# Hybrid block and two attention layers on one core: maxima spread by transfers, triangle products as first term, weights' splits moved or given to GpSimd

## The reference

```python
h = rms_norm(x, g); u, z_a, q, k, v, o, z_b, gates, g_a, g_b = split(h @ w_in)
y_a = (mix(window_means(u) - u) * pool_scale) * silu(z_a)
q, k = silu(conv5(q, k))
hb = mlstm(q, k, v, i, f) + flip(mlstm(flip(...)))        # 4 heads of 256
y_b = rms(hb) * g * sigmoid(o) * silu(z_b)
x = x + rms_norm((sigmoid(g_a) * (y_a @ Wa) + sigmoid(g_b) * (y_b @ Wb)) @ w_out)
# layer e: 6 heads with a window of 128, 6 heads with distance bias, 4 heads on the memory
# layer o: 12 heads with a forget bias (running sum of log sigmoid), 4 heads on the memory
x = x + (attention * silu(z)) @ w_out_layer
```

## Time and profile before

| | |
|---|---|
| median of 3 runs | 1219.95 us |
| lowest and highest run | 1217.41, 1223.23 us |
| the profiled execution's own time | 1218.77 us |
| its span, first to last instruction | 1216.9 us |
| TensorE busy | 1175.4 us, 97% |
| VectorE, ScalarE, GpSimd busy | 633.7, 568.6, 132.3 us |
| HBM read and written | 102.55 and 2.12 MB |

### The profile page before, as it was taken

How to read it: one execution, slowest core, us unless ns; L and a number is a source line. 1 busy time by engine, 2 the same in 40 slices (tenths; PEclk the granted TensorE clock), 3 DMA queues, 4 the chain that set the end, 5 groups by cost and what they waited for, 6 DMA issues and landing times.

```text
span 1216.9 us, 15215 instructions
## 1 busy us (share of the span) xinstructions
PE 1175.4 (97%) x5970; PEld 952.1 (78%) x5970; DVE 633.7 (52%) x1174; ACT 568.6 (47%) x1013; POOL 132.3 (11%) x146
## 2 busy tenths in 40 slices
PE   5999999999999999999999999899999999999998
PEld 4887888888876777788788888677788788877777
DVE  5485423588533454434547663787445565256631
ACT  4433431243335444544335565677434576366630
POOL 1000000000000000000000004334220000522522
PEclk9999999999999999999999999999999999999999
DMA  5233223332221221143335233212223233122221
GB/s 182 94 99 103 73 101 104 104 98 79 101 70 36 69 69 35 49 140 104 119 144 127 78 104 69 62 45 70 68 72 106 70 104 102 64 70 70 79 70 69
DMA packets 106703, 105.65 MB, mean 87 GB/s; under 512 B 17788, under 2 KB 92924, under 8 KB 106632
## 3 DMA queue, kind: packets, MB, share of 16 engines
q1 hardware_dynamic: 104984, 98.46, 25.8%
q10 hardware_dynamic: 1648, 6.23, 1.4%
HBM read 102.55 MB, written 2.12 MB: 86 GB/s over the span
## 4 chain that ended last, share of the span: by engine, by line
PE 90%; DVE 5%; ACT 3%; issue 1%; DMA 0%; DVEq 0%; ACTq 0%
PE acc L1522 23%; PE acc L1524 23%; PE acc L1523 23%; PE acc L1858 3%; PE aux L1884 3%; PE aux L1872 2%; PE aux L1696 2%; PE aux L1522 2%; PE aux L1524 2%; PE aux L1523 2%; PE aux L1710 2%; DVE wlo L995 2%; ACT whi L633 1%; PE acc L1863 1%; PE aux L1612 1%
## 5 line engine op out<-in xcount | busy, mean ns | idle before, releaser
L1522 PE MATMUL acc<-ht_hi,whi 128*128 128x512 f32 x736 | 293.4, 399 | 8.9 <-DVE wlo L995 7.9
L1523 PE MATMUL acc<-ht_lo,whi 128*128 128x512 f32 x736 | 287.8, 391 | 0.0
L1524 PE MATMUL acc<-ht_hi,wlo 128*128 128x512 f32 x736 | 287.7, 391 | 0.0
L995 DVE TENSOR_TENSOR wlo<-raw,whi 128x2048 fp32r<-128x2048 f32 x71 | 162.3, 2288 | 156.2 <-ACT whi L633 150.4
L1522 PEld LDWEIGHTS acc<-ht_hi,whi 128*128 128x128 f32 x736 | 139.0, 189 | 40.4 <-DVE wlo L995 9.3
L1523 PEld LDWEIGHTS acc<-ht_lo,whi 128*128 128x128 f32 x736 | 139.0, 189 | 30.0 <-issue 1.9
L1524 PEld LDWEIGHTS acc<-ht_hi,wlo 128*128 128x128 f32 x736 | 139.0, 189 | 29.3
L633 ACT ACTIVATE whi<-raw 128x2048 fp32r<-128x2048 f32 x71 | 135.3, 1910 | 50.8 <-DMA raw<-w_in_dram 22.9
L579 POOL TENSOR_SCALAR whi<-raw 128x512 fp32r<-128x512 f32 x64 | 43.4, 679 | 1029.0 <-DMA raw<-e_w_in_dram 758.7
L1522 PE MATMUL acc<-whi,ht_hi 128*128 128x512 f32 (+1 forms) x224 | 84.1, 375 | 0.8 <-DVE gbT L1246 0.8
L580 POOL TENSOR_TENSOR wlo<-raw,whi 128x512 fp32r<-128x512 f32 x64 | 83.4, 1303 | 5.3
(11 more groups left out here) (226 smaller groups left out, 1852.0 us busy)
## 6 DMA issues: line engine op xcount, KB each, us to landing
raw<-w_in_dram SPq DMA_DIRECT2D x72, 512.0 KB, 4.4
raw<-o_w_in_dram SPq DMA_DIRECT2D x28, 512.0 KB, 4.5
raw<-e_w_in_dram SPq DMA_DIRECT2D x14, 512.0 KB, 5.0
raw<-w_proj_pool_dram SPq DMA_DIRECT2D x8, 512.0 KB, 4.0
raw<-w_proj_mlstm_dram SPq DMA_DIRECT2D x8, 512.0 KB, 4.4
raw<-w_out_dram SPq DMA_DIRECT2D x8, 512.0 KB, 4.4
raw<-o_w_out_dram SPq DMA_DIRECT2D x8, 512.0 KB, 4.7
raw<-e_w_in_dram SPq DMA_DIRECT2D x14, 256.0 KB, 3.8
```

The lines of the kernel that those rows point to most:

```text
L995: v.tensor_tensor(wlo[:, slot, :], raw[:, slot, :], whi[:, slot, :].bitcast(F32), ALU.subtract).then_inc(w_split, 1)
L1522: mm(out_, w_hi_, x_hi, start=first, stop=False)
L1523: mm(out_, w_hi_, x_lo, start=False, stop=False)
L1524: return mm(out_, w_lo_, x_hi, start=False, stop=last)
```

## The change

- The maxima: after the scans VectorE signals `rowmax_ready`; SP stores the 64 x 512 rows to DRAM after the loads of w_proj_pool. After the loads of v it spreads head 0's two rows to 128 partitions into `rowmax_all`, and for each later head it does the same between the loads of O(h) and ZB(h), after waiting until all decay arguments of the head before are made. `rowmax_hi`, `rowmax_lo`, their split and the spreading products are gone, with two waits of TensorE. VectorE reads the maxima from `rowmax_all`.
- The triangles: `causal(p)` waits for the pair two before and, in layer o, writes the triangle products as the first term of the diagonal block. A step issues `causal` of both pairs, then the scores of both. Scores in layer o are cut at the diagonal block and are added.
- The rest of unit 1 is made ahead of the gate rows.
- The mix is evicted into eight tiles `mixT` of their own, without waiting for heads; the rest of g_a's second unit comes before the eight rests.
- In stage ozb the head and the rest of O(h+1) stand behind the head's normalisation, on both engines.
- The memory values' unit is split in iteration t = 1, and all first transposes stand after the first half of the values.
- GpSimd splits the first q/k unit of layer o.

```diff
@@ -148,12 +148,12 @@
         xnrow = at("xnrow", [P, TT, D], R0)
-        rowmax_hi = at("rowmax_hi", [64, S], CST + 7 * K, F32R)
-        rowmax_lo = at("rowmax_lo", [64, S], CST + 9 * K, F32R)
+        rowmax_all = at("rowmax_all", [P, 2, S], CST + 7 * K)
         zaT = at("zaT", [P, KT, S], R0)
...
         win_t = at("win_t", [P, 4, S], R3 + 5 * K)
+        mixT = at("mixT", [P, KT, S], R1)
         grow = at("grow", [P, 7, S], R2 + 2 * K)
@@ -190,6 +190,7 @@
 
+        rowmax_dram = nc.dram_tensor("rowmax_rows", (64, S), F32, kind="Internal").ap()
         csum_dram = nc.dram_tensor("csum_rows", (C_HEADS, S), F32, kind="Internal").ap()
@@ -228,12 +229,13 @@
         gm_ready = sem("gm_ready")
-        rowmax_split = sem("rowmax_split")
+        rowmax_ready = sem("rowmax_ready")
+        rowmax_out = sem("rowmax_out")
+        rowmax_in = sem("rowmax_in")
         last_rows = sem("last_rows")
...
         floor_ready = sem("floor_ready")
-        mbc_ready = sem("mbc_ready")
         s_ready = sem("s_ready")
@@ -324,7 +326,7 @@
 
-        BY_POOL = {plan["gates"][0], plan["o_f"][0]}
+        BY_POOL = {plan["gates"][0], plan["o_f"][0], plan["o_qk"][0]}
         for name in ("e_z", "e_out", "o_z", "o_out"):
@@ -478,11 +480,24 @@
             stage("pa", wview(A["w_proj_pool"][0]), 0)
+            sp.wait_ge(rowmax_ready, 1)
+            sp.dma_start(rowmax_dram, rowmax[:]).then_inc(rowmax_out, 16)
+
+            def spread_rowmax(h):
+                if h:
+                    sp.wait_ge(arg_ready, 2 * TT * h)
+                for d in range(2):
+                    r = 32 * d + h
+                    sp.dma_start(rowmax_all[:, d, :], rowmax_dram[r:r + 1, :].to_broadcast([P, S])).then_inc(rowmax_in, 16)
             stage("qk", W1, COL_QK)
             stage_wide("v", W1, COL_V, 4)
+            sp.wait_ge(rowmax_out, 16)
+            spread_rowmax(0)
             n = plan["ozb"][0]
...
                 load(W1, h * UC + COL_O, 2 * h + n)
+                if h:
+                    spread_rowmax(h)
                 load(W1, h * UC + COL_ZB, 2 * h + n + 1)
@@ -607,6 +622,7 @@
             split_narrow(plan["o_f"][0], C_HEADS, [(0, 0, C_HEADS)])
+            split(plan["o_qk"][0])
             for name in ("o_z", "o_out"):
@@ -707,7 +723,7 @@
             for j in range(KT):
-                head(win_t[:, j % 4, :], op_hi[:, j, :])
+                head(mixT[:, j, :], op_hi[:, j, :])
             weight_heads(n0 + 2)
@@ -780,7 +796,6 @@
                     evac(a, a % 2, half, ogT[:, 2 * h + half:2 * h + half + 1, :], ACT.Sigmoid)
-                weight_heads(n0 + 2 * h + 2)
                 for t in range(TT):
@@ -796,6 +811,7 @@
                 nc.scalar.activation(small[:, 8:12], small[:, 4:8], ACT.Exp, scale=-0.5).then_inc(hrs_ready, 1)
+                weight_heads(n0 + 2 * h + 2)
                 if h + 1 < HEADS:
@@ -848,7 +864,7 @@
                     root(t - 1)
-                if t == 2:
+                if t == 1:
                     weight_heads(n0 + 5)
@@ -1041,6 +1057,7 @@
             G = lambda i, lo=0, hi=64: grow[lo:hi, i, :]
+            weight_rests(1)
             dve.wait_ge(acc_ready, 2)
@@ -1089,10 +1106,9 @@
             step(v.tensor_tensor_scan(rowmax[32:64, ::-1], back, back, FLOOR, ALU.max, ALU.bypass))
+            dve.sem_inc(rowmax_ready, 1)
             v.tensor_tensor(G(5, 64, 128), G(4), rowmax[:], ALU.add).then_inc(gm_ready, 1)
             v.tensor_copy(ident_r[:], ident[:])
-            step(v.tensor_copy(rowmax_hi[:], rowmax[:]))
-            v.tensor_tensor(rowmax_lo[:], rowmax[:], rowmax_hi[:].bitcast(F32), ALU.subtract).then_inc(rowmax_split, 1)
             weight_rests(n0 + 5)
@@ -1108,15 +1124,14 @@
                     j = 2 * g + half
-                    dve.wait_ge(hi_ready, 8 + j - 3)
-                    tile_written(v.scalar_tensor_tensor(win_t[:, j % 4, :], acc[:, 2 * s + half, :], V("pool_scale", j),
+                    tile_written(v.scalar_tensor_tensor(mixT[:, j, :], acc[:, 2 * s + half, :], V("pool_scale", j),
                                                         zaT[:, j, :], ALU.mult, ALU.mult))
...
                 dve.sem_inc(acc_free, 1)
-                for j in (2 * g, 2 * g + 1):
-                    rest(win_t[:, j % 4, :], op_hi[:, j, :], op_lo[:, j, :])
-
             n0, _, _ = plan["ga"]
+            weight_rests(n0 + 1)
+            for j in range(KT):
+                rest(mixT[:, j, :], op_hi[:, j, :], op_lo[:, j, :])
             weight_rests(n0 + 3)
@@ -1170,9 +1185,9 @@
                     w = hi - lo
-                    dve.wait_ge(mbc_ready, h + 1)
+                    dve.wait_ge(rowmax_in, 32 * (h + 1))
                     mask = masks1[:, 0, 0:w] if d == 0 else masks1[:, 1, S - w:S]
-                    v.scalar_tensor_tensor(decay[:, seen["arg"] % 4, 0:w], aux[:, d, lo:hi], gcol[:, j, d, h:h + 1],
+                    v.scalar_tensor_tensor(decay[:, seen["arg"] % 4, 0:w], rowmax_all[:, d, lo:hi], gcol[:, j, d, h:h + 1],
                                            mask, ALU.subtract, ALU.max).then_inc(arg_ready, 1)
@@ -1197,7 +1212,6 @@
             for h in range(HEADS):
-                weight_rests(n0 + 2 * h + 2)
                 for t in range(TT):
@@ -1215,6 +1229,7 @@
                 ins.then_inc(hbn_ready, 1)
+                weight_rests(n0 + 2 * h + 2)
                 if h + 1 < HEADS:
@@ -1675,17 +1690,9 @@
                     pe.wait_ge(hb_ready, TT * h)
-                    if h > 1:
-                        pe.wait_ge(t_ready, 16 + 2 * (h - 1))
                 else:
...
                     pe.wait_ge(floor_ready, 2)
-                for d in range(2):
-                    r = 32 * d + h
-                    one_row = ident_r[0:64, r:r + 1].to_broadcast([64, P])
-                    mm(aux[:, d, :], one_row, rowmax_hi[0:64, :], start=True, stop=False)
-                    ins = mm(aux[:, d, :], one_row, rowmax_lo[0:64, :], start=False, stop=True)
-                ins.then_inc(mbc_ready, 1)
                 score_tiles(h, (0, 1))
@@ -1723,7 +1730,6 @@
             pe.wait_ge(consts_in, 32)
-            pe.wait_ge(rowmax_split, 1)
             scores(0)
@@ -1778,12 +1784,11 @@
                                 ins.then_inc(tr_ready, 1)
-                first_transposes(range(3))
                 n, a = n0 + 1, a0 + 1
...
                     if t:
-                        first_transposes((3,))
+                        first_transposes(range(TT))
                     for k in range(KT):
@@ -1846,22 +1851,29 @@
                 def logits(p):
+                    first = pairs[p][0]
+                    forget = first.bias is not None and first.bias[0] == "forget"
+                    ends = [c for c in range(2 * P, first.keys, 2 * P)] + [first.keys]
+                    if forget and first.keys - P not in [0] + ends:
+                        ends.insert(-1, first.keys - P)
+                    c = 0
+                    for end in ends:
+                        for e, job in enumerate(pairs[p]):
+                            (qt, qp), (kt_, kp) = job.q, job.k
+                            k0 = P * job.k0
+                            ins = mm(logit_bank(p, e)[:, c:end], qk[qp:qp + HD2, qt, P * job.t:P * job.t + P],
+                                     (mkT if job.bias is None else qk)[kp:kp + HD2, kt_, k0 + c:k0 + end],
+                                     start=not forget, stop=not forget or end == first.keys)
+                        c = end
+                    ins.then_inc(logit_ready, 1)
+
+                def causal(p):
+
                     if p >= 2:
                         pe.wait_ge(nm_ready if pairs[p - 2][0].bias is not None else pr_ready, 2 * (done + p - 1))
-                    first = pairs[p][0]
-                    forget = first.bias is not None and first.bias[0] == "forget"
-                    for c in range(0, first.keys, 2 * P):
-                        w = min(2 * P, first.keys - c)
-                        for e, job in enumerate(pairs[p]):
-                            (qt, qp), (kt_, kp) = job.q, job.k
-                            k0 = P * job.k0 + c
-                            ins = mm(logit_bank(p, e)[:, c:c + w], qk[qp:qp + HD2, qt, P * job.t:P * job.t + P],
-                                     (mkT if job.bias is None else qk)[kp:kp + HD2, kt_, k0:k0 + w],
-                                     start=True, stop=not (forget and c + w == job.keys))
-                    if forget:
-                        for e, job in enumerate(pairs[p]):
-                            ins = mm(logit_bank(p, e)[:, job.keys - P:job.keys], ident_r[:], causal_r[:], start=False, stop=True)
-                    ins.then_inc(logit_ready, 1)
+                    for e, job in enumerate(pairs[p]):
+                        if job.bias is not None and job.bias[0] == "forget":
+                            mm(logit_bank(p, e)[:, job.keys - P:job.keys], ident_r[:], causal_r[:], start=True, stop=False)
 
```

(2 more changed lines are left out.)

## The result

The changed kernel takes 1186.47 us, the median of four runs (1186.28 to 1189.16), against 1218.68 us of the kernel before beside it (1215.85 to 1223.23). The ratio is 0.9731 with an interval of 0.9706 to 0.9757. The forecast was 1191.5.

What follows compares the result with a forecast made beforehand. TensorE, busy 1175.4 of 1216.9 us, was taken as the bound. Terms 2.9 + 1.7 + 7.4 + 1.7 + 4.8 + 6.0 + 0.9 + 2.1 = 27.5 us off 1218.8 gave 1191.3, stated as 1191.5; range 1186 to 1201.

Steps and rivals of the forecast that it cites:

- split behind normalisation: Output gate's weight split after the head's normalisation: all four waits for `hrow` go, 7.4 us, at worst two thirds.
- maxima: Maxima spread by transfers: 1.22 us for each of three heads and 1.1 for the first, 4.8 together.
- triangles: Triangles as first term in layer o: 0.5 us in each of 12 steps, 6.0 us, at worst 4.0.
- first rest: First weight's rest ahead of the gate rows: u starts 2.9 us earlier; the clock's first fall, 1.7, counted separately.
- clock: Two of five half-clock stretches go, ahead of u and at the `hrow` wait: 1.7 us each, bounds 0 and 1.7.
- Rival B: Fewer clock falls than forecast: the three kept ones vanish too, 1186 us; chance 0.08.
- D: Values still wait, GpSimd is late, or late decay factors stop the scores: about 5 us less, 1196.5; chance 0.11.
- F: The maxima's broadcasts compete with weight loads, 512 KB more per head: 1193 us at most; chance 0.04.
- C: Triangles give little since VectorE's chain, not TensorE, sets the step: 6 us less, 1197.5; chance 0.1.
- E: Waiting for both pairs ahead of the scores closes a ring of late scores and VectorE minima: 1225 us; chance 0.01.
- Transposes and the GpSimd weight: Later transposes at layer e's memory values: 0.9 us, bounds 0 and 1.9; o_qk weight by GpSimd: 2.1, bounds 0 and 2.2.
- Rival A: The clock falls again in other places, behind remaining or new waits, two more falls: 1195 us; chance 0.2.

Runs made afterwards that it cites:

- four parts undone: Changed kernel with the first weight's rest, o_qk by GpSimd, later transposes and eight mixed tiles undone at once: 1198.3 us, ratio to before 0.9823.

## Why the prediction was right or wrong

Each row: what the prediction gave, what the traces' product starts gave, what undoing the part gave at full clock. The changed kernel stands at 1184.4 (eight runs).

| part | forecast | by starts | undone, full clock |
|---|---|---|---|
| split behind normalisation | 7.4 | 8.5 | 9.3 |
| maxima | 4.8 | 5.1 | 6.2 |
| triangles | 6.0 | 5.9 | 5.9 |
| first rest, GpSimd weight, transposes, tiles | 5.9 | 6.0 | 5.3 |
| sum without the clock | 24.1 | 25.5 | 26.7 |
| clock | 3.4 | 7.2 by the runs' mean clocks | |

At full clock the change is worth 1209.6 - 1184.4 = 25.2 us. The mean clock is known to 0.0005, 0.6 us in one run, and the start of the kernel varies by as much, so I take the last column as good to some 0.5 us a row; its sum is 1.5 above the 25.2, which four such errors can make. Within that the parts add up and none covers for another.

- **The falls of the clock: the step that failed.** Keeping three falls ("at most three stretches at 1.2 GHz") and 1.7 us each for two that go took the falls of one profiled execution as a property of the kernel. The runs of before lost 10.5 us to the clock on average (time multiplied by one minus the clock), those of the changed kernel 3.3: 7.2 us, not 3.4. By the medians it is 7.0: before lies 9.1 above its 1209.6 and the changed kernel 2.1 above its 1184.4. So 3.6 of the 5.0 us missed are the clock. Another 1.1 are sizes (24.1 forecast, 25.2 at full clock), 0.2 the rounding from 1191.3 to 1191.5 and 0.1 the base. The profiled execution did have three falls and took 1189.16; three of the first four runs, the median's among them, had a clock of 0.998 or 0.999, which in two other profiles (maxima by TensorE, the changed kernel once more) goes with a single fall.
- **Which falls went.** The prediction put 1.7 us on the fall behind `hrow` and 1.7 on the one ahead of u. With the four waits for `hrow` back, the runs lost 3.3 us to the clock, as much as the changed kernel; with the waits of 4.26, 2.97 and 2.17 us back, 8.4. The means of the other edited kernels, which have none of those waits, lie between 2.1 and 5.4, so only the second is clear of chance: some 5 of the 7.2 us belong to those three waits. That the fall at 960.7 is gone from the profile after is chance: its wait of 1.47 us is still there, and six of the ten profiles after the change that have it show a fall behind it.
- **Rival B**, the fewer falls at 1186, came nearest and had a chance of 0.08. Its number was partly luck: the falls did not all vanish, and the 1.1 us of sizes made up for one that stayed. The spread of the runs before (1217.41 to 1223.23) already held the hint: most of it is a differing number of falls on top of some 1209.6 us of work and waits.
- **Split behind the normalisation.** The mechanism was right. Each wait was taken at its idle entry of 1.86; it is worth 2.14, since records overlap and the products resume late. That is 1.1 us of the miss. No wait took its place: the decay factors, 2.7 us later, were covered, and so D was wrong.
- **Maxima.** Right, 5.1 by starts instead of 4.8. The transfers take 5.1 us, above the row that I took, and hide as said: F was wrong.
- **Triangles.** Right to 0.1 us, with 0.49 for the 0.5 a step; the run of four triangles takes 0.49 us (1084.86 to 1085.35) for the 0.43. The four extra changes of shape that the step named are three by the count above; the saving did not rest on their number. C and E fall: no scores of layer o wait. The waits for both pairs are 1.4 us in layer e, inside the 0 to 2 given, and most of it comes back at `zT`: without those of layer e the kernel takes 1184.0 at full clock, against 1184.4.
- **First rest.** 2.9 us, and its fall of 1.6 too. In the experiment without it the fall came back.
- **Transposes and the GpSimd weight.** 0.8 for 0.9 and 2.3 for 2.1. The weight is ready at 912.7, TensorE comes at 913.2, and GpSimd's pieces took 0.62 and 1.29 (the last 0.63 and 1.31) beside the `ht_lo` of VectorE, undisturbed as assumed.
- **Mixed tiles.** Nothing, as said.
- **Rival A** was half right: in the profiled execution two falls came at 755.9 and 783.2 in layer e, where there had been one. The second profile of the same kernel has neither. But of the twelve profiles of the changed kernel and its edits nine have the first and nine the second, and of the kernel before there is a single profile, so whether the change makes falls there more frequent stays open.

What stays open is which executions fall where. Apart from the start (7.4 and 7.8 us for the first `xnrow`), the waits of the changed kernel's two profiles are the same to 0.1 us, and the falls are not.

## What to carry to other kernels

Multiply each run's time by its mean granted clock before comparing kernels that are within one per cent: here that took 23 runs of one kernel from a spread of 8.0 us to one of 3.1 (1207.7 to 1210.8), their group means to 0.2, and let single parts of 2 us be read. Forecast the clock's falls as an expectation over executions, from the runs' mean clocks, and not from the stretches of one trace. Price a wait from the start of one product to that of the next less the normal pitch, not by its idle entry; and ask of a split given to GpSimd what VectorE does beside it, not only whether it is in time.

## What the runs showed of the hardware

- **A wait does not decide a fall, but no fall came without one.** In the thirteen profiles every fall inside the kernel (the last 1.2 us left out) begins during a wait of TensorE of 1.47 us or more, or at most 1.5 us behind it. The reverse does not hold: 2.0 us at the mix was followed by 3.41 us at 1.2 GHz in four of ten profiles, 1.47 us at the third q/k unit of layer o in seven of eleven, 1.9 us for `hrow` once in eight, 2.16 us at the first q/k unit of layer o not before and yes with four parts undone, and 2.97 us at the transposes likewise. Only the 4.26 us ahead of u's first product was followed by a fall in both profiles that have it. The Trainium skill (TensorE: Matmul & The Clock Gate, Part 1) says of the slow matmuls at the start of a kernel that their number differs between runs of one kernel; these traces show the same of the later falls.
- **A change of product shape** costs TensorE some 0.19 us at the spreading products (0.09 ahead of the first product of the new shape and 0.10 behind it) and 0.15 to 0.18 us in layer o's steps.
- **VectorE beside GpSimd.** Scaling one f32 tile by a column, with one tile read from SBUF, went from 0.75 to 1.84 us beside a GpSimd split, whose own pieces grew from 0.62 to 1.07 and from 1.29 to 2.15, while `ht_lo`, which reads PSUM and SBUF, left GpSimd at 0.62 and 1.29. So a single tile read from SBUF does not by itself keep an instruction clear of GpSimd. The Trainium skill (SBUF — State Buffer, Who interferes with whom) says that such a scaling can contend where it enters a two-port mode. The trace shows the contention, not the mode.
